# Second attention layer: query tiles of 16 rows x 8 columns, keys and values in bands of 8 columns

## The reference, cut to what matters

```
q, k, v, g = split(u @ w_in, 4)
first_row = clip(r - 4, 0, 16 - 8);  first_col = clip(c - 8, 0, 64 - 16)
s      = q . k * 64**-0.5 + rel_bias[head, row_k - r + 7, col_k - c + 15]   (keys of the window)
s_ctx  = q . kc * 64**-0.5
p      = softmax([s, s_ctx]);   o = p @ [v, vc]
y      = (o * silu(g)) @ w_out
h      = layer_norm(alpha * h + gate * y)
```

## Time and profile before

| | |
|---|---|
| median of 3 runs | 2031.76 us (2030.78 to 2032.8) |
| profiled execution | 2033.18 us, span 2031.3 us |
| granted TensorE clock, mean | 0.992 |
| TensorE matmul busy | 1973.5 us, 97% |
| VectorE / ScalarE / GpSimd busy | 1076.8 / 828.8 / 834.8 us |
| eight pairs of layer B | about 1351 to 1936 us of the span |
| GpSimd bias adds L855 / L856 | 93.1 / 82.1 us, 96 each |
| VectorE logits waiting for bias | 15.8 us, 7 times |

### The profile page before, as it was taken

The page is one execution under the profiler, slowest core; times in us unless marked ns, Lnnn a source line. Parts: engine busy times, 40 slices in busy tenths (PEclk is TensorE's granted clock), DMA queues, the critical chain, the costliest instruction groups (busy, mean ns, idle before and its releaser), DMA issues.

```text
span 2031.3 us, 36948 instructions
## 1 busy us (share of the span) xinstructions
PE 1973.5 (97%) x14892; PEld 1636.7 (81%) x14892; DVE 1076.8 (53%) x2229; ACT 828.8 (41%) x1641; POOL 834.8 (41%) x624
## 2 busy tenths in 40 slices
PE   7999999999999999999999999999999999999996
PEld 6888888888887888888888788778888888888784
DVE  5566556766855665556666733734334334344626
ACT  4110110110126466556677610735555555555601
POOL 3433333333345712212122635545435435434746
PEclk9999999999999999999999999999999999999997
DMA  4432332332221401110001333221111111111343
GB/s 161 134 103 86 101 96 81 114 94 83 94 94 63 157 20 37 35 35 30 22 30 35 135 97 112 79 83 53 42 52 53 43 52 52 43 52 52 110 135 120
DMA packets 51063, 156.02 MB, mean 77 GB/s; under 512 B 5584, under 2 KB 9296, under 8 KB 50768
## 3 DMA queue, kind: packets, MB, share of 16 engines
q1 hardware_dynamic: 49888, 152.40, 22.6%
q10 hardware_dynamic: 1008, 1.27, 0.2%
HBM read 132.94 MB, written 20.71 MB: 76 GB/s over the span
## 4 chain that ended last, share of the span: by engine, by line
PE 64%; DVE 3%; POOL 2%; issue 2%; ACT 2%; DMA 1%; DVEq 0%; SPq 0%; POOLq 0%; ACTq 0%
PE psum L915 16%; PE psum L916 14%; PE psum L917 14%; PE psum L1104 8%; PE psum L1051 6%; PE psum L1067 5%; PE psum L924 1%; POOL w_lo L732 1%; DVE prob_t L1824 1%; DMA w_raw<-weights_in 1%; POOL rstd L755 0%; DVE logits L1802 0%; ACT logits L1385 0%; PE psum L1078 0%; POOL out_tile L897 0%
## 5 line engine op out<-in xcount | busy, mean ns | idle before, releaser
L915 PE MATMUL psum<-u_hi,w_hi 128*128 128x512 f32 (+1 forms) x1440 | 545.0, 378 | 2.6 <-DVE u_lo L1689 2.6
L916 PE MATMUL psum<-u_lo,w_hi 128*128 128x512 f32 (+1 forms) x1440 | 526.0, 365 | 0.0
L917 PE MATMUL psum<-u_hi,w_lo 128*128 128x512 f32 (+1 forms) x1440 | 525.3, 365 | 0.0
L730 POOL CAST w_hi<-w_raw 128x1024 fp32r<-128x1024 f32 x140 | 155.0, 1107 | 820.3 <-DMA w_raw<-weights_in 820.2
L732 POOL TENSOR_TENSOR w_lo<-w_raw,w_hi 128x1024 fp32r<-128x1024 f32 x140 | 349.2, 2494 | 11.2
L915 PEld LDWEIGHTS psum<-u_hi,w_hi 128*128 128x128 f32 x1440 | 272.5, 189 | 55.3 <-DVE u_lo L1689 4.4
L917 PEld LDWEIGHTS psum<-u_hi,w_lo 128*128 128x128 f32 x1440 | 272.9, 190 | 45.0
L916 PEld LDWEIGHTS psum<-u_lo,w_hi 128*128 128x128 f32 x1440 | 273.1, 190 | 38.6
L1385 ACT ACTIVATE logits<-logits,neg_max 128x640 f32<-128x640 f32 (+2 forms) x288 | 225.9, 785 | 71.6 <-DVE neg_max L1802 70.2
L1394 ACT ACTIVATE logits<-logits,row_rec 128x640 f32<-128x640 f32 (+1 forms) x288 | 218.0, 770 | 0.0
L1408 ACT ACTIVATE prob_t<-psum 128x320 f32<-128x320 f32 (+1 forms) x288 | 118.9, 413 | 235.8 <-PE psum L1067 235.6
(11 more groups left out here) (165 smaller groups left out, 3047.2 us busy)
## 6 DMA issues: line engine op xcount, KB each, us to landing
w_raw<-weights_in SPq DMA_DIRECT2D x140, 512.0 KB, 3.5
w_ada<-w_ada_in SPq DMA_DIRECT2D x48, 512.0 KB, 3.5
residual<-act_buf SPq DMA_DIRECT2D x4, 2048.0 KB, 7.4
tab<-bias_tab_in SPq DMA_DIRECT2D x16, 496.5 KB
res<-residual SPq DMA_DIRECT2D x26, 256.0 KB, 3.4
y_all<-staged SPq DMA_DIRECT2D x24, 256.0 KB, 4.6
act_buf<-x_t_in SPq DMA_DIRECT2D x8, 512.0 KB, 13.4
staged<-a_y SPq DMA_DIRECT2D x6, 640.0 KB, 2.9
```

Of the source, the lines that this page charges most:

```text
L730: pool.tensor_copy(w_hi[:, slot, :], w_raw[:, slot, :]).then_inc(w_hi_done, 1)
L915: pe.matmul(out, wh, xh, start=first, stop=False)
L916: pe.matmul(out, wh, xl, start=False, stop=False)
L917: return pe.matmul(out, wl, xh, start=False, stop=last)
```

## The change

Tiles of layer B become 16 rows by 8 columns, tile t = column band t. q, k and v of the latent tokens are written in band order (band, row, column) when they are evicted, so a tile's keys are bands t - 1 to t + 1, contiguous; tile 0 and tile 7 have two bands (512 keys with the context). `a_tile` of layer A becomes `key_span` and serves both layers. Values are 10 blocks a pair: three "t" chunks at the start, five groups of two in tiles 3 to 5.

The bias has three planes (first, inner, last band) that are all held at once, with one mask `b_mask` of 7 x 128 per partition, loaded by DMA. The table (now 31 x 31 with zeros, 489 elements a partition) is divided by the score scale in place (two instructions a pair), and the scale moves from the keys to the factor of the logits. Planes are built by one add of 128 elements for each band and head: 4, 6 and 4 adds. GpSimd's order in a pair j becomes: plane 1, split, plane 2, split, scaling and plane 0 of pair j + 1, split, split. Pair 0 has all three built up front.

Gate chunks of layer B cover column halves (16 rows by 32 columns) of all rows. The late chunk of the last pair so reads all of `u_lo`; the loads of y wait for its parts: pairs 0 to 2 for the first, 3 to 5 for the second, and GpSimd's split of pair 6 for the whole.

```diff
-    def b_window(rows, half, cb):
-        return rows.rearrange(...)[:, 4 * half:4 * half + KEY_ROWS, KEY_COL[cb]:KEY_COL[cb] + KEY_COLS]
+    def in_bands(rows, n):
+        return rows[:, 0:S].rearrange("p (b r c) -> p r b c", c=BAND, r=ROWS)[:, n * ROWS // 2:(n + 1) * ROWS // 2]
+    def by_rows(ap):
+        return ap.rearrange("p (r b c) -> p r b c", b=S // P, c=BAND)
+    def half_columns(rows, n):
+        return rows[:, 0:S].rearrange("p (r c) -> p r c", c=GRID)[:, :, n * GRID // 2:(n + 1) * GRID // 2]
...
-V_TILE, V_TURNS, V_TILES = (0, 3), (2, 3), (S // P + C // P, 18)
+V_TILE, V_TURNS, V_TILES = (0, 3), (2, 2), (S // P + C // P, S // P + C // P)
-LAST_BIAS_USE = ((1, 6), (1, 7), (0, 0), (0, 2), (0, 3), (0, 4))
+LAST_BIAS_USE = (0, 6, 7)
...
         def load_y(layer, loaded, spans, chunks):
-            sp.wait_ge(pj_done, chunks)
             sp.wait_ge(y_stored, 16 * STAGED * (layer + 1))
+            if chunks is not None:
+                sp.wait_ge(pj_done, chunks)
             for k in range(STAGED):
+                if chunks is None and k % 3 == 0:
+                    sp.wait_ge(late_part, k // 3 + 1)
...
-                step(pool.tensor_tensor(dst, src, cm, ALU.add))
-                pool.tensor_tensor(dst, dst, rm, ALU.add).then_inc(bias_ready, 1)
+                if j:
+                    pool.wait_ge(logit_done, STEP0[1] + (j - 1) * B_STEPS + 2 * LAST_BIAS_USE[b] + h + 1)
+                for g in range((LAT_KEYS - lo) // P):
+                    at = (1 - BIAS_FIRST[b] - g) * BAND
+                    ins = pool.tensor_tensor(dst[:, g], tab[h][:, :, at:at + BAND][:, ::-1, ::-1], mask[:, g], ALU.add)
+                ins.then_inc(bias_ready, 1)
...
         for j in range(PAIRS):
-            bias_tile(j, 2)
+            if j:
+                bias_tile(j, 1)
             if more:
                 split(n + W_SLOTS)
-            bias_tile(j, 3)
-            bias_tile(j, 4)
+            if j:
+                bias_tile(j, 2)
             if more:
                 split(n + 1 + W_SLOTS)
-            bias_tile(j, 5)
                 first_bias(j + 1)
                 split(n + 2 + W_SLOTS)
                 if j + 2 < PAIRS:
                     split(n + 3 + W_SLOTS)
...
+                        if layer == 1 and c.kind == "g":
+                            xs = half_columns(u_hi[:, k, :], c.n), half_columns(u_lo[:, k, :], c.n)
...
-                    for cb in range(4):
-                        dst = b_vt[:, cb * HALF + c.n * C:cb * HALF + (c.n + 1) * C].rearrange("p (r c) -> p r c", c=KEY_COLS)
-                        ins = act.activation(dst, src..., ACT.Copy)
+                    ins = act.activation(in_bands(b_vt, c.n), by_rows(src), ACT.Copy)
...
-            dve.tensor_tensor_reduce(logits..., ps_score..., add, -1.0,
-                                     start, ALU.add, ALU.min, neg_max[:, n:n + 1]).then_inc(logit_done, 1)
+            dve.tensor_tensor_reduce(logits..., ps_score..., add,
+                                     (-1.0, -Q_SCALE)[layer], start, ALU.add, ALU.min, neg_max[:, n:n + 1]).then_inc(logit_done, 1)
```

More of the change, by code:

```diff
@@ L105 @@
 B_START = [("q", 0), ("k", 0), ("v", 0), ("k", 2), ("v", 2), ("q", 1), ("k", 1), ("v", 1), ("g", 0), ("g", 1)]
-B_START += [("t", n) for n in range(5)]
+B_START += [("t", n) for n in range(3)]
 STARTS = (A_START, B_START)
@@ L113, in lay_out @@
 def lay_out(layer, unit, index):
-    turns = ([(0, 4), (4, 4), (8, 2)], [(0, 4), (4, 4), (8, 4), (12, 4), (16, 2)])[layer]
+    turns = [(0, 4), (4, 4), (8, 2)]
     stages = []
@@ L708, in _ @@
                 store_y(1, j)
[L709 removed]
+        load_y(1, y_loaded, Y_FIRST[1], None)
         load_early(1)
@@ L892, in _ @@
                     split(n + 3 + W_SLOTS)
+            else:
+                split_y(1, *range(KT - 1))
+                split_late(1, *range(KT - 1))
+                split(BO_UNIT + 2)
         def add_row(t):
@@ L1096, in outputs @@
                     consumed(pe, c)
-            if layer == 0:
-                v, tiles = av[pair // 4], a_tile(t)[2]
-            else:
-                v, tiles = bv[pair % 2], [t % 4 * 4 + t // 4 + n for n in range(3)] + [16, 17]
+            v, tiles = (av[pair // 4], bv[pair % 2])[layer], key_span(t)[2]
             for c, tile in enumerate(tiles):
@@ L1185, in attention @@
                         if part[0].kind == "g":
-                            work(layer, [part])
+                            mm = work(layer, [part])
+                            if layer == 1 and part[2] < KT:
+                                mm.then_inc(late_part, 1)
                             continue
@@ L1343, in take @@
                 y = y_buf[layer][c.pair % 2]
+                if layer == 1:
+                    out, src = half_columns(y, c.n), src.rearrange("p (r c) -> p r c", c=GRID // 2)
+                else:
+                    out = y[:, span]
                 if c.n == 0 and c.pair >= 2:
@@ L1347, in take @@
                     act.wait_ge(res_stored, 16 * (3 + 2 * layer))
-                act.activation(y[:, span], src, ACT.Tanh, scale=0.5).then_inc(gate_tanh, 1)
+                act.activation(out, src, ACT.Tanh, scale=0.5).then_inc(gate_tanh, 1)
             elif layer == 0:
@@ L1792, in logit @@
             if layer == 0:
-                start, m0 = sink_neg[:, 2 * pair + h:2 * pair + h + 1], a_tile(t)[3]
+                start, m0 = sink_neg[:, 2 * pair + h:2 * pair + h + 1], key_span(t)[3]
                 add = a_mask[:, m0:m0 + KEYS - c0]
@@ L2053, in shape_tables @@
     p = np.arange(P)
-    rr, qq = p // 16, p % 16
-    row_mask = np.zeros((P, 2, KEY_ROWS))
-    for half in range(2):
-        first = np.clip(8 * half + rr - 4, 0, ROWS - 8)[:, None]
-        key = 4 * half + np.arange(KEY_ROWS)
-        row_mask[:, half] = np.where((key >= first) & (key < first + 8), 0, MASKED)
-    col_mask = np.zeros((P, 3, KEY_COLS))
-    for kind, cb in enumerate((0, 1, 3)):
-        first = np.clip(cb * 16 + qq - 8, 0, GRID - 16)[:, None]
-        key = KEY_COL[cb] + np.arange(KEY_COLS)
-        col_mask[:, kind] = np.where((key >= first) & (key < first + 16), 0, MASKED)
-    t["row_mask"], t["col_mask"] = row_mask, col_mask
+    rr, qq = (n[:, None, None, None] for n in (p // BAND, p % BAND))
+    key_r, key_c = np.arange(ROWS)[:, None], np.arange(BAND)
+    b_mask = []
+    for band, (lo, hi) in zip((0, 1, GRID // BAND - 1), ((0, 2), (0, 3), (GRID // BAND - 2, GRID // BAND))):
+        key_col = np.arange(lo, hi)[:, None, None] * BAND + key_c
+        first_row = np.clip(rr - 4, 0, ROWS - 8)
+        first_col = np.clip(band * BAND + qq - 8, 0, GRID - 16)
+        seen = (key_r >= first_row) & (key_r < first_row + 8) & (key_col >= first_col) & (key_col < first_col + 16)
+        b_mask.append(np.where(seen, 0, MASKED).reshape(P, -1))
+    t["b_mask"] = np.concatenate(b_mask, axis=1)
     col = np.arange(P)
```

145 lines of the change are left out of this document (65 added, 80 removed).

## The result

The changed kernel takes 2066.06 us (median of 4 runs, 2063.2 to 2068.68), the kernel before on the same chip 2032.28 (4 runs, 2030.78 to 2033.6): ratio 1.0166, 95% interval 1.0152 to 1.0179. It is 34 us slower where 1.8 us less was forecast. The profiled execution took 2065.64 us, span 2063.8, mean granted clock 0.991.

A forecast was written before the change was run, and what follows sets the result against it. TensorE was taken to bound the kernel. Gains of 15.0 us less an added wait of 13.2 left 1.8 us less: 2031.4, brought to the median 2030.0 us, range 2020 to 2037.

The forecast's parts named there:

- the dear adds: Rival at layer B's passages between pairs: six serial small GpSimd adds, at 0.8 us each, give 2042 us; chance 0.16.
- TensorE bounds the kernel, and only added work or waits in layer B move the end: Layer B: TensorE busy for all 76.7 us of a pair, so savings on other engines are worth nothing by themselves.
- Gains, 15.0 us: TensorE in layer B: 7.4 from shorter edge tiles, 6.2 and 1.4 from fewer value blocks turned; 13 to 17 us.
- Contiguous keys and column halves at nothing, bound 2.6 us: Layer B's score and gate matmuls: contiguous keys gain nothing, gates reading runs of 32 lose nothing, at most 2.6 us.
- The wait, 13.2 us: Passages between layer B pairs: inner bias built behind a weight split, TensorE loses 2.2 us at six of seven.
- its two links: TensorE's stops at a passage: about 1.3 us ahead of the output products, the rest (0.9) at the turn.
- the 0.45 us add: GpSimd's bias add of 128 elements at a passage: 0.45 us, 0.41 from start to start.
- the one gap that the prediction named as a sign against itself: Passages between layer B pairs: TensorE showing one gap or none, instead of two, would prove the prediction wrong.
- Late loads of y at nothing, larger evictions at nothing: Layer B: y's late pieces need 5.2 of 6.0 us, q, k, v evictions use idle time; both cost nothing.

The follow-up runs named there:

- run 4: Changed kernel with 480 unused bytes a partition where the masks stood, and the next pair's plane 1 bias built ahead of the last weight split: 2026.16 us.
- run 1: Changed kernel with 480 unused bytes a partition where the two removed masks stood, so later arrays regain their old addresses: 2042.34 us.
- run 10: Kernel before, with the loads of row_mask and col_mask moved behind c_in in ScalarE's row of loads: 2036.15 us, ratio 1.0019.
- run 3: Kernel before with 32 unused bytes behind the small arrays, so its big arrays start 32 over a multiple of 64: 2058.72 us.
- run 7: Kernel before with 32 unused bytes between act_buf and x_hi, shifting streamed operands but not weights: 2058.59 us, ratio 1.0129.
- run 6: run 4 with layer B's gate matmuls reading 512 neighbouring columns instead of 16 rows of 32 (output not the reference's): 2021.35 us.

## Why the prediction was wrong

The steps in their order, with what each measured; attention B is read from the table under run 4. The measured time is 29 us past the upper end of the range, and no rival of the prediction, the dear adds included, names what took most of it.

- **TensorE bounds the kernel, and only added work or waits in layer B move the end.** This is the step that failed. That TensorE is the bound held. But the prediction went on that "the end moves only by what TensorE executes, or by a wait that TensorE did not have before", and put the time of every matmul that the change doesn't edit at that of before, with no reason given. Its gains, moves and wait were all looked for in layer B. The change also moves the arrays that the matmuls read, all over the program, and a queue at its start: two arrays less ahead of w_ada, two loads less on ScalarE, and neither got a line of its own. The runs showed in its place that an unedited matmul of 512 columns goes from 226.7 to 233.3 ns with the start of its operand. Price of the first: 23.7 us (changed kernel less run 1), of the second about 4 (run 10).
- **Gains, 15.0 us.** The size was right. Before less run 4 in attention B is 11.6, with some 3.8 lost to the column halves in it (3.4 by the table's projections): 15.0 to 15.4. Output products 3.2 (3.5 forecast); transposes with the turns 6.4 + 1.7, scores 3.5, which share out the rest otherwise than forecast.
- **Contiguous keys and column halves at nothing, bound 2.6 us.** Wrong for the gates, and past the bound: 3.8 us. The bound scaled 5 ns at 384 keys, read from two layers with 64 rows of operand; the real figure is 10 ns at 512 columns. The scores of an inner tile take 0.97 us in run 4, 0.99 before, 48 times: contiguous keys may have given 0.9 us, which no run separates.
- **The wait, 13.2 us.** Its place, its two links and the 0.45 us add were right (450 ns, spacing 0.41). From the output products on, in the passage shown above, VectorE's logits of the second head began at +9.67 (forecast 9.53) and TensorE's turn at +13.75 (13.6). TensorE's list has 13.6, in run 1 14.1; by run 1 against run 4 it is 15.8 in the intervals, and up to 3.2 more where the clock was low. That the sum came so near is in part luck: five passages lost 2.0 to 2.2 us as forecast, and the sixth, 3.3 in one wait, shows the one gap that the prediction named as a sign against itself.
- **Late loads of y at nothing, larger evictions at nothing.** Held: in the last pair TensorE waits only for turned probabilities, 1.7 us at the longest (2.0 before). The q and k evictions on ScalarE read 585 and 596 ns as before, and v's, now one of 512, 588 (0.6 forecast).

The account, beside the 33.8 us measured:

| cause | us | shown by |
|---|---|---|
| start of x, m, g, u at 32 over a multiple of 64 | +23.7 | changed kernel less run 1; 27.1 in run 3, 27.1 in run 7 |
| two loads fewer ahead of c_in | +4 | run 10 |
| less work in layer B | -15.4 | before less run 4, intervals (11.6), and the gates' 3.8 |
| gates by column halves | +3.8 | run 6, intervals |
| wait for the middle bias | +15.8 | run 1 less run 4, intervals |
| granted clock in attention B | +3.2 | windows of run 1; the first stretch stands beside the sixth wait, the cause of the second is open |

The sum is 35.1. The addresses give 23.7 here and 27.1 in the kernel before. A part of the difference can be read: the column-half gates take 238.2 ns in run 1 and 237.7 in the changed kernel, so they lose nothing by the start, while the same 384 matmuls in row order go from 228.3 to 233.3 in the kernel before and run 3 (six pairs of layer B, 270 intervals): 1.9 us. The rest, which also holds more time at the lower clock in the changed kernel than in run 1, isn't separated. Without its first two rows the sum is 7.4, some 2 us past the upper end of the range and not 29: the mechanism that was worked out carries the smaller part of the miss, and what decided was outside it.

That the address sets the pace is shown (runs 1, 3, 7). Why 64 over a multiple of 128 costs a third, why 256-column matmuls gain, why weights and operands cost alike, and why the pace in the attention layers differs from that in the pooling block is open. The Trainium skill (SBUF — State Buffer, Operand start alignment) requires only a multiple of the element size, 4 bytes here, and says of itself that it is about legality, not speed; every kernel here obeys it.

## What to carry to other kernels

When a diff removes or resizes a buffer, work out the start of every array that TensorE streams, weights included, before pricing anything else; keep both at a multiple of 128 bytes, which for fp32r was as good here as 256 and better than 64 or 32, and put odd-sized small arrays behind them. When it removes a transfer, ask what is queued behind it and now starts earlier. And compare the mean of an untouched matmul form before and after first: if it moved, the cause isn't in the changed stage.

## What the runs showed of the hardware

- In the pooling block, back-to-back fp32r matmuls of 128x128 by 512 columns start every 226.7 ns (544 cycles at 2.4 GHz) with operands and weights at multiples of 128 bytes, every 228.9 with operands at 64 over one, every 233.3 (560 cycles) with operands or weights at 32 over a multiple of 64. In attention A the mean goes from 229.5 to 233.2 only, in B from 228.2 to 233.2 (before and run 3). At 256 columns, over the whole program, by the operands' start: 119.5, 116.9 and 117.0.
- An operand of 16 runs of 32 floats costs 10 ns in 512 columns (runs 4 and 6), and then its start at 32 over a multiple of 64 costs nothing more (238.2 and 237.7 ns).
- Beside a wait of 2.9 to 3.6 us that ended near 19 us TensorE was granted 1.2 GHz for 3.4 or 6.8 us, in each of the six kernels in which that wait occurred and in none of the six others. The same stood beside the 3.1 to 3.4 us of the sixth passage, in all three kernels that have it.
